# A two-layer streaming encoder step on one core: the gathered rows and the dense stage's middle rows get padded rows, so that each k starts at another distance from the weights

## The chip, the cores and the metric

The kernel runs on one core of one Trainium2 chip. The time is the device time of one execution in microseconds (us). TensorE is called PE in the rows, its weight loads PEld, VectorE DVE, ScalarE ACT, GpSimd POOL.

## The reference, cut to what matters

Two layers over 320 tokens (256 of a prompt, 64 of a running stream), model width 1024, everything in float32. Each layer mixes tokens (a short convolution beside a gated linear attention) between one input and one output projection, normalises, and then mixes channels: layer 0 with a dense SwiGLU of width 3584, layer 1 with 8 experts of the same width of which each token uses two.

```python
def _swiglu(x, w_gate, w_up, w_down):
    return (jax.nn.silu(x @ w_gate) * (x @ w_up)) @ w_down

def _moe(x, router, w_gate, w_up, w_down):
    ...
    logits = (xf @ router).astype(jnp.float32)
    top_v, top_i = lax.top_k(logits, TOP_K)
    gates = jax.nn.softmax(top_v, axis=-1)
    ...
    for e in range(N_EXPERTS):
        y = y + combine[:, e:e + 1] * _swiglu(xf, w_gate[e], w_up[e], w_down[e])
```

## The kernel before, in words

**Products in three parts.** A float32 product is made of three matmuls on rounded operands (type fp32r): high part by high part, and each high part by the other operand's rest. `raw` is a ring of 6 weight units of 2048 words per partition that SP loads; ScalarE rounds a unit into the ring `whi` (3 units), VectorE writes the rest into `wlo` (3 units), and TensorE reads both.

**Mixer and dense stage (16 + 42 + 16 units).** The weights are the stationary operand (128 x 128, loaded before each matmul), the tokens' transposed activations `xh`, `xl` (or `y_split`) the moving one with 320 columns. `split_product` (lines 619 to 625) issues the three matmuls of a pair: line 622 high by high, 623 high weights by low input, 624 low weights by high input. In the dense stage (`dense_mixer`) a chunk of 512 middle columns takes four gate and up units and two down units; the down units' moving operand is `hh[:, k, :]` and `hl[:, k, :]`, k from 0 to 3, which ScalarE (line 1258) and VectorE (line 1695) write.

**Expert stage.** Four passes of `pair` (experts two at a time, 128 gathered rows each, 14 chunks of 512 middle columns a pass). Here the gathered rows are the stationary operand and the weights the moving one, with 512 columns:

```python
for j in range(4):
    k = 4 * half + j
    ...
    wh, wl = slot(whi, n, SPLIT, 4)[:, j, :], slot(wlo, n, SPLIT, 4)[:, j, :]
    xh_k, xl_k = (xg[:, k, m, P * a:P * a + P] for m in range(2))
    pe.matmul(bank[:], xh_k, wh, start=k == 0, stop=False)                # line 959
    pe.matmul(bank[:], xh_k, wl, start=False, stop=False)                 # line 960
    mm = pe.matmul(bank[:], xl_k, wh, start=False, stop=k == KT - 1)      # line 961
```

A chunk is gate (24 matmuls), up (24), and the down product of the chunk before (24, line 984, stationary `hT_hi`/`hT_lo`, moving `whi`/`wlo`), with four transposes of 128 columns (line 997) between the two halves of the gate. At the end of a pass four gathers (line 934) make the next pass's `xg`: ScalarE evicts the high part (`hi_of_pair`, line 1297), VectorE the rest (`lo_of_pair`, line 1851). The order on each engine is written out by hand; semaphores tie the engines together.

**Where the operands lie.** Within a partition, `xg` has 2048 bytes a k (high part of 256 words, then the low part; expert `a` 512 bytes in). A unit of `whi` or `wlo` is 8192 bytes: in the expert gate and up units a k is 2048 bytes, in the dense down units too, in the mixer and the dense gate and up units 1024 bytes. `xh`, `xl`, `y_split`, `hh` and `hl` have 320 words, 1280 bytes, a k. Tiles start at multiples of 32 bytes. `raw`, `whi`, `wlo`, `xh`, `hh`, `hl`, `xg` and `hT_hi` all start 128 bytes past a multiple of 256. `w_split`, the stationary operand of the low-rank product (lines 800 and 801), has 128 bytes a k and starts behind `prm`, whose 110 words are rounded to 448 bytes, so it lies 32 bytes off the others' raster of 64.

Of the kernel before, what the change touches and what calls it, by code (L numbers as in the profile page):

```python
# [17 lines left out]
F32 = mybir.dt.float32  # L18
F32R = mybir.dt.float32r
I32 = mybir.dt.int32  # L20
ALU = mybir.AluOpType
ACT = mybir.ActivationFunctionType
AXX = mybir.AxisListType.X

P = 128
# [8 lines left out]
def hybrid_stream_step(nc, x_prompt, x_sample, cache_conv, state_gla, ln_mix_g, ln_mix_b, w_in, w_alpha2,  # L34
# [3 lines left out]
    DEPTH, D, IN_COLS = w_in.shape  # L38
    SEQ, DEC = x_prompt.shape[1], x_sample.shape[1]
    T = SEQ + DEC  # L40
# [4 lines left out]
    E = moe_router.shape[2]  # L45
# [3 lines left out]
    KT = D // P  # L49
    TT = -(-T // P)  # L50
# [70 lines left out]
    with ctx:  # L121
# [54 lines left out]
        def sbm(name, shape, dt=F32):  # L176
# [11 lines left out]
                                                                                        k=KT)  # L188
# [22 lines left out]
        def sbd(name, shape, dt=F32):  # L211
            return dense.enter_context(nc.sbuf_tensor(name, shape, dt))

        silu_g = sbd("silu_g", [P, 2, T])
        hid = sbd("hid", [P, 2, T])
        hh = sbd("hh", [P, 4, T], F32R)
        hl = sbd("hl", [P, 4, T], F32R)
        dense.close()
        early.close()
        late = ExitStack()  # L220
# [2 lines left out]
        def sbl(name, shape, dt=F32):  # L223
            return late.enter_context(nc.sbuf_tensor(name, shape, dt))

        def sbx(stack, name, shape, dt=F32):
            return stack.enter_context(nc.sbuf_tensor(name, shape, dt))
# [12 lines left out]
        acc_s.close()  # L240
        y_out = sbl("y_out", [P, TT, D])
        pair_s = ExitStack()
        xg = sbx(pair_s, "xg", [P, KT, 2, 2 * P], F32R)
        pair_s.close()
        ys_hi = sbl("ys_hi", [P, D], F32R)
        ys_lo = sbl("ys_lo", [P, D], F32R)
        sbl("xg_rest", [P, KT * 4 * P - 2 * D])
        sg = sbl("sg", [P, 2, 512])
        hm = sbl("hm", [P, 2, 512])
        hT_hi = sbl("hT_hi", [P, 2, 4, P], F32R)  # L250
# [2 lines left out]
        gT_hi = sbl("gT_hi", [P, TT * P], F32R)  # L253
# [13 lines left out]
        comb = sbl("comb", [P, TT, E])  # L267
        qpos = sbl("qpos", [P, TT, E])
        over_n = sbl("over_n", [P, 2 * E])
        over_k = sbl("over_k", [P, 3])  # L270
        src_at = sbl("src_at", [P, SRC])
        src_on = sbl("src_on", [P, SRC])
        slot_of = sbl("slot_of", [P, ROOM, SRC])
# [6 lines left out]
        row_in = sbl("row_in", [P, TT, SLOTS])  # L280
        row_at = sbl("row_at", [P, 3, TT])
        gate_at = sbl("gate_at", [P, 3, TT])
        in_6 = sbl("in_6", [P, TT])
        row_i = sbl("row_i", [P, 3, TT], I32)
        ctl_f = sbl("ctl_f", [P, 16])
        ctl = sbl("ctl", [1, 16], I32)
        rs_tok = sbl("rs_tok", [P, TT])
        acc_sum = sbl("acc_sum", [P, TT])
        ys_sums = sbl("ys_sums", [P, 4])
        ys_sum = sbl("ys_sum", [P, 1])  # L290
        sq_sums = sbl("sq_sums", [P, TT, 2])
        neg_mean = sbl("neg_mean", [P, TT])
        eps_1 = sbl("eps_1", [P, TT])
        pick_g = x[:, :, :].rearrange("p k t -> p (k t)")[:, 2 * D:2 * D + TT * P].rearrange("p (t s) -> p t s", t=TT)
        gb_rows = x[:, :, :].rearrange("p k t -> p (k t)")[:, 0:2 * D].rearrange("p (a d) -> p a d", a=2)
        lgT = hm[0:E, 0, 0:T]
# [321 lines left out]
        def _(pe):  # L618
# [320 lines left out]
            def pair(i, steps, first=False):  # L939
                unit, job = 0, GATHERS  # L940
                for part, c, half in steps:
# [3 lines left out]
                    if part in ("gate", "up"):  # L945
# [7 lines left out]
                        for j in range(4):  # L953
                            k = 4 * half + j
                            if j % 2 == 0:
                                pe.wait_ge(lo_ready, upto(2 * n + j // 2 + 1, i, 2 * PER_PAIR))
                            wh, wl = slot(whi, n, SPLIT, 4)[:, j, :], slot(wlo, n, SPLIT, 4)[:, j, :]
                            xh_k, xl_k = (xg[:, k, m, P * a:P * a + P] for m in range(2))
                            pe.matmul(bank[:], xh_k, wh, start=k == 0, stop=False)  # L959
                            pe.matmul(bank[:], xh_k, wl, start=False, stop=False)  # L960
                            mm = pe.matmul(bank[:], xl_k, wh, start=False, stop=k == KT - 1)  # L961
                            if j % 2:
                                mm.then_inc(unit_used, 1)
# [70 lines left out]
            def combine():  # L1034

                def newest(d, t):
                    out, tokens = ps[OUT_BANKS[t][d]][:], slice(P * t, P * t + P)
                    pe.matmul(out, gT_hi[:, tokens], ys_hi[:, HALVES[d]], start=False, stop=False)
                    pe.matmul(out, gT_lo[:, tokens], ys_hi[:, HALVES[d]], start=False, stop=False)
                    pe.matmul(out, gT_hi[:, tokens], ys_lo[:, HALVES[d]], start=False, stop=True).then_inc(r_tok, 1)  # L1040

                pe.wait_ge(ys_lo_ready, 1)
                for t in range(TT):
                    newest(0, t)

                pe.wait_ge(sum_ready, 1)
                for t in range(TT):
                    tokens = slice(P * t, P * t + P)
                    pe.matmul(ps[4][:, t:t + 1], gT_hi[:, tokens].bitcast(F32), ys_sum[:], start=True, stop=False)
                    mm = pe.matmul(ps[4][:, t:t + 1], gT_lo[:, tokens].bitcast(F32), ys_sum[:], start=False, stop=True)  # L1050
                mm.then_inc(mean_tok, 1)
                pe.wait_ge(ys_lo_ready, 2)
                for t in range(TT):
                    newest(1, t)
# [17 lines left out]
        def _(act):  # L1072
# [221 lines left out]
                act.activation(ident_r[:], ident[:], ACT.Copy).then_inc(ys_ready, 1)  # L1294

            def hi_of_pair(g, bank):
                act.activation(xg[:, 2 * g:2 * g + 2, 0, :], bank[:].rearrange("p (k s) -> p k s", k=2), ACT.Copy
                               ).then_inc(xg_hi_ready, 1)

            def pair(i, steps, first=False):  # L1300
# [77 lines left out]
        def _(dve):  # L1378
# [342 lines left out]
            def router():  # L1721
# [22 lines left out]
                    return n  # L1744

                dve.wait_ge(stored, 16 * LAYER_STORES * DEPTH)
                dve.memset(acc_sum[:], 0.0).then_inc(m_hid, 1)
                step(dve.memset(lg[:], 0.0))
                dve.wait_ge(lg_done, 1)
                step(dve.tensor_copy(lgT, ps[0][0:E, 0:T]))  # L1750
# [97 lines left out]
                    table(g_tab, csh)  # L1848

            def lo_of_pair(g, bank):  # L1850
                dve.tensor_tensor(xg[:, 2 * g:2 * g + 2, 1, :], bank[:].rearrange("p (k s) -> p k s", k=2),
                                  xg[:, 2 * g:2 * g + 2, 0, :].bitcast(F32), ALU.subtract).then_inc(job_read, 1)

            def make_pick(i, tab=q_tab):

# [5 lines left out]
            def rows_of_tokens(c, step):  # L1861
# [14 lines left out]
                elif c == 1:  # L1876
                    step(dve.scalar_tensor_tensor(out=g_tab[:], in0=row_of[:], scalar=0.0, in1=g_tab[:], op0=ALU.is_gt,
                                                  op1=ALU.mult))
                    step(dve.tensor_reduce(row_2, row_of[:], AXX, ALU.max))
                    step(dve.tensor_reduce(row_1, row_of[:], AXX, ALU.add))  # L1880
                    step(dve.tensor_tensor(row_1, row_1, row_2, ALU.subtract))
                    step(dve.tensor_tensor(row_in[:], row_of[:], row_2.unsqueeze(2).to_broadcast(full), ALU.is_equal))
                    step(dve.tensor_tensor(row_in[:], row_in[:], g_tab[:], ALU.mult))
                elif c == 2:
                    step(dve.tensor_reduce(gate_2, row_in[:], AXX, ALU.add))
                    step(dve.tensor_reduce(gate_1, g_tab[:], AXX, ALU.add))
                    step(dve.tensor_tensor(gate_1, gate_1, gate_2, ALU.subtract))
                    step(dve.tensor_scalar(in_6[:], qpos[:, :, E - 2], 1.0, None, ALU.is_ge))
                    step(dve.scalar_tensor_tensor(out=in_6[:], in0=qpos[:, :, E - 2], scalar=float(P), in1=in_6[:],
                                                  op0=ALU.is_le, op1=ALU.mult))  # L1890
                    step(dve.scalar_tensor_tensor(out=row_6, in0=qpos[:, :, E - 2], scalar=over_k[:, 1:2], in1=in_6[:],
                                                  op0=ALU.add, op1=ALU.mult))
                elif c == 3:
                    step(dve.tensor_tensor(gate_6, comb[:, :, E - 2], in_6[:], ALU.mult))
                    step(dve.tensor_tensor(gate_1, gate_1, gate_6, ALU.add))
                    step(dve.tensor_tensor(row_1, row_1, row_6, ALU.add))
                    step(dve.tensor_scalar(row_at[:], row_at[:], -1.0, 0.0, ALU.add, ALU.max))
                    dve.tensor_copy(row_i[:], row_at[:]).then_inc(rows_known, 1)
                elif c == 4:
                    for t in range(TT):  # L1900
                        ins = dve.tensor_scalar(pick_g[:, t, :], slot_no[:], qpos[:, t, E - 1:E], comb[:, t, E - 1:E],
                                                ALU.is_equal, ALU.mult)
                    ins.then_inc(rows_known, 1)
# [57 lines left out]
            def final_norm():  # L1961
                halves = [slice(512 * d, 512 * d + 512) for d in range(2)]
                for d, cols in enumerate(halves):
# [2 lines left out]
                                             in1=ys_hi[:, cols].bitcast(F32), op0=ALU.mult, op1=ALU.subtract,  # L1966
                                             accum_out=ys_sums[:, 2 + d:3 + d]).then_inc(ys_lo_ready, 1)
                dve.wait_ge(ys_lo_ready, 2)
                dve.tensor_reduce(ys_sum[:], ys_sums[:], AXX, ALU.add).then_inc(sum_ready, 1)
                dve.tensor_scalar(acc_sum[:], acc_sum[:], -1.0 / D, None, ALU.mult).then_inc(sum_ready, 1)  # L1970
                dve.wait_ge(sum_ready, 2)
                dve.wait_ge(mean_tok, 1)
                dve.scalar_tensor_tensor(out=neg_mean[:], in0=ps[4][:, 0:TT], scalar=-1.0 / D, in1=acc_sum[:],
                                         op0=ALU.mult, op1=ALU.add).then_inc(mean_ready, 1)
                dve.wait_ge(mean_ready, 1)
                dve.wait_ge(gb_landed, 32)
# [65 lines left out]
```

## Time and profile before

| | |
|---|---|
| median of 3 runs | 1600.7 us (1599.65 to 1600.92) |
| the profiled execution's own time | 1599.57 us |
| its span, first to last instruction | 1597.9 us |
| PE busy | 1575.9 us, 99% of the span, 8661 matmuls |
| PEld busy | 1395.9 us (87%) |
| DVE / ACT busy | 1244.9 us (78%) / 1022.2 us (64%) |
| granted clock of TensorE | 0.998 of the full 2.4 GHz |

A matmul's own duration (389 ns for 512 columns) is longer than the time from its start to the next one's start, because matmuls are pipelined; what a stage costs is read from the starts. Weight loads run beside the matmul before.

### The profile page before, as it was taken

Reading aid. Unit: us, or ns where it says so; the run is one execution under the profiler, and the core shown is the slowest. Engines: PE = TensorE matmul, PEld = TensorE weight load, DVE = VectorE, ACT = ScalarE, POOL = GpSimd, SP = SyncE. Lnnn points to the kernel's source line nnn. Section 1 sums busy time; section 2 is a strip of 40 time slices with the busy share of each in tenths; the row PEclk is TensorE's granted clock in tenths of the full one; section 3 lists DMA queues with packets and bytes.
Section 4 is the critical chain, followed back from the end, with each engine's and each line's share of the span. In section 5 each row is a group of like instructions: output and inputs, shape, how many; then the busy total and the mean of one; then the engine's idle time right before and its main releaser. Section 6 shows DMA issues by size and latency. Waiting matters only on the chain.

```text
span 1597.9 us, 23664 instructions
## 1 busy us (share of the span) xinstructions
PE 1575.9 (99%) x8661; PEld 1395.9 (87%) x8661; DVE 1244.9 (78%) x1416; ACT 1022.2 (64%) x1178; POOL 45.1 (3%) x72
## 2 busy tenths in 40 slices
PE   9999999999999999999999999999999999999997
PEld 8998999999989998888888888888888888888885
DVE  5577545444575678999998989988988988998996
ACT  4454333333354557788787778777778777877875
POOL 1002000000030010000000000000000001000100
PEclk9999999999999999999999999999999999999999
DMA  9524644444434344999998999998999999999992
GB/s 284 185 80 139 237 158 144 145 157 136 154 106 132 106 139 164 376 373 386 370 383 329 383 370 375 381 382 320 381 380 365 385 379 350 382 395 378 389 394 77
DMA packets 226576, 445.40 MB, mean 279 GB/s; under 512 B 10547, under 2 KB 72705, under 8 KB 226433
## 3 DMA queue, kind: packets, MB, share of 16 engines
q1 hardware_dynamic: 224288, 434.16, 75.4%
q0 software_dynamic: 2192, 9.98, 1.7%
q8 instruction: 58, 0.95, 0.2%
q14 instruction: 38, 0.30, 0.1%
HBM read 438.59 MB, written 8.67 MB: 280 GB/s over the span
## 4 chain that ended last, share of the span: by engine, by line
PE 95%; DVE 3%; ACT 1%; issue 1%; DVEq 0%; POOL 0%; ACTq 0%; POOLq 0%
PE ps L984 18%; PE ps L959 12%; PE ps L961 12%; PE ps L960 12%; PE ps L622 11%; PE ps L623 11%; PE ps L624 11%; PE ps L997 1%; PE ps L934 1%; PE ps L654 1%; DVE wlo L1388 1%; DVE x L1471 1%; DVE xl L1462 0%; DVE x L1453 0%; PE ps L1029 0%
## 5 line engine op out<-in xcount | busy, mean ns | idle before, releaser
L1388 DVE TENSOR_TENSOR wlo<-raw,whi 128x1024 fp32r<-128x1024 f32 x672 | 778.5, 1220 | 43.8 <-ACT whi L1083 42.6
L1083 ACT ACTIVATE whi<-raw 128x1024 fp32r<-128x1024 f32 x672 | 676.9, 1055 | 60.8 <-PE ps L984 51.9
L959 PE MATMUL ps<-whi,xg 128*128 128x512 f32 x896 | 354.2, 395 | 0.0
L961 PE MATMUL ps<-whi,xg 128*128 128x512 f32 x896 | 349.8, 390 | 0.0
L960 PE MATMUL ps<-wlo,xg 128*128 128x512 f32 x896 | 349.2, 390 | 0.0
L622 PE MATMUL ps<-xh,whi 128*128 128x320 f32 x832 | 260.2, 313 | 4.5 <-DVE xl L1462 3.8
L1383 DVE TENSOR_TENSOR wlo<-raw,whi 128x2048 fp32r<-128x2048 f32 x73 | 167.4, 2295 | 124.8 <-ACT whi L1079 124.8
L624 PE MATMUL ps<-xh,wlo 128*128 128x320 f32 x832 | 257.3, 309 | 0.0
L623 PE MATMUL ps<-xl,whi 128*128 128x320 f32 x832 | 257.3, 309 | 0.0
L961 PEld LDWEIGHTS ps<-whi,xg 128*128 128x128 f32 x896 | 168.3, 188 | 35.7
L960 PEld LDWEIGHTS ps<-wlo,xg 128*128 128x128 f32 x896 | 168.5, 188 | 33.6
L959 PEld LDWEIGHTS ps<-whi,xg 128*128 128x128 f32 x896 | 168.4, 188 | 33.3
L1079 ACT ACTIVATE whi<-raw 128x2048 fp32r<-128x2048 f32 x73 | 139.1, 1906 | 60.6 <-PE ps L624 56.1
L622 PEld LDWEIGHTS ps<-xh,whi 128*128 128x128 f32 x832 | 156.2, 188 | 9.4 <-issue 4.2
L623 PEld LDWEIGHTS ps<-xl,whi 128*128 128x128 f32 x832 | 156.3, 188 | 0.2
L624 PEld LDWEIGHTS ps<-xh,wlo 128*128 128x128 f32 x832 | 156.2, 188 | 0.0
L984 PE MATMUL ps<-whi,hT_hi 128*128 128x512 f32 x440 | 135.6, 390 | 0.0
L984 PE MATMUL ps<-wlo,hT_hi 128*128 128x512 f32 x440 | 135.6, 389 | 0.0
L984 PE MATMUL ps<-whi,hT_lo 128*128 128x512 f32 x440 | 135.5, 389 | 0.0
L984 PEld LDWEIGHTS ps<-whi,hT_lo 128*128 128x128 f32 x440 | 82.6, 188 | 17.2
L984 PEld LDWEIGHTS ps<-wlo,hT_hi 128*128 128x128 f32 x440 | 82.6, 188 | 17.2
L1337 ACT ACTIVATE hT_hi<-ps 128x512 fp32r<-128x512 f32 x56 | 33.5, 599 | 99.9 <-PE ps L997 99.5
(327 smaller groups left out, 1496.5 us busy)
## 6 DMA issues: line engine op xcount, KB each, us to landing
raw<-in_moe_w_gate SPq DMA_DIRECT2D x112, 1024.0 KB, 7.5
raw<-in_moe_w_up SPq DMA_DIRECT2D x112, 1024.0 KB, 7.8
raw<-in_moe_w_down SPq DMA_DIRECT2D x112, 1024.0 KB, 7.3
raw<-in_w_in SPq DMA_DIRECT2D x23, 1024.0 KB, 6.2
raw<-in_ffn_w_gate SPq DMA_DIRECT2D x14, 1024.0 KB, 5.0
raw<-in_ffn_w_up SPq DMA_DIRECT2D x14, 1024.0 KB, 5.1
raw<-in_ffn_w_down SPq DMA_DIRECT2D x14, 1024.0 KB, 5.0
raw<-in_w_out SPq DMA_DIRECT2D x8, 1024.0 KB, 5.1
```

The lines of the kernel that those rows point to most:

```text
L622: pe.matmul(out, wh, hi, start=start and j == 0, stop=False)
L623: pe.matmul(out, wh, lo, start=False, stop=False)
L624: mm = pe.matmul(out, wl, hi, start=False, stop=stop and j == len(pairs) - 1)
L959: pe.matmul(bank[:], xh_k, wh, start=k == 0, stop=False)
L960: pe.matmul(bank[:], xh_k, wl, start=False, stop=False)
L961: mm = pe.matmul(bank[:], xl_k, wh, start=False, stop=k == KT - 1)
L984: mm = pe.matmul(ps[4 + d][:], hT[:, c % 2, k, :], slot(w, n, SPLIT, 2)[:, j, 512 * d:512 * d + 512], start=fc == 0 and k == 0 and hT is h ...
L1079: act.activation(flat(whi, n, SPLIT), flat(raw, n, RAW), ACT.Copy).then_inc(hi_ready, 2)
L1083: act.activation(part(whi, n, SPLIT, h), part(raw, n, RAW, h), ACT.Copy).then_inc(hi_ready, 1)
L1337: act.activation(hT_hi[:, c % 2, :, :].rearrange("p f s -> p (f s)"), bank[:], ACT.Copy).then_inc(hT_hi_ready, 1)
L1383: dve.tensor_tensor(flat(wlo, n, SPLIT), flat(raw, n, RAW), flat(whi, n, SPLIT).bitcast(F32), ALU.subtract).then_inc(lo_ready, 2)
L1388: dve.tensor_tensor(part(wlo, n, SPLIT, h), part(raw, n, RAW, h), part(whi, n, SPLIT, h).bitcast(F32), ALU.subtract).then_inc(lo_ready, 1)
```

## The change: padded rows, and small tiles put together

`xg` gets 16 more words a k (2112 bytes instead of 2048), with high and low parts side by side in one row of 4 x 128 words; its readers and writers address the same words in the new form. `hh` and `hl` get 16 more words a k (1344 bytes instead of 1280). `xg_rest`, which keeps the room of `xg`, grows with it, so all tiles behind it lie 512 bytes further on. Some small tiles are put together (`over_k` with `in_6`; `rs_tok`, `eps_1`, `neg_mean`, `acc_sum` and `sq_sums`; `ys_sums` with `ys_sum`), which frees bytes that rounding to 32 took. No instruction, wait, count or shape of an operand changes; `xh`, `xl`, `y_split`, `hT_hi`, `hT_lo` and the weight rings keep their steps.

```diff
-        hh = sbd("hh", [P, 4, T], F32R)
-        hl = sbd("hl", [P, 4, T], F32R)
+        hh = sbd("hh", [P, 4, T + 16], F32R)[:, :, 0:T]
+        hl = sbd("hl", [P, 4, T + 16], F32R)[:, :, 0:T]
...
-        xg = sbx(pair_s, "xg", [P, KT, 2, 2 * P], F32R)
+        xg = sbx(pair_s, "xg", [P, KT, 4 * P + 16], F32R)
...
-        sbl("xg_rest", [P, KT * 4 * P - 2 * D])
+        sbl("xg_rest", [P, KT * (4 * P + 16) - 2 * D])
...
-        over_k = sbl("over_k", [P, 3])
+        over_in = sbl("over_in", [P, 3 + TT])
+        over_k, in_6 = over_in[:, 0:3], over_in[:, 3:3 + TT]
...
+        rs_parts = sbl("rs_parts", [P, 6, TT])
+        rs_tok, eps_1, neg_mean, acc_sum = (rs_parts[:, n, :] for n in range(4))
+        sq_sums = rs_parts[:, 4:6, :].rearrange("p a t -> p (a t)").rearrange("p (t a) -> p t a", a=2)
+        ys_parts = sbl("ys_parts", [P, 5])
+        ys_sums, ys_sum = ys_parts[:, 0:4], ys_parts[:, 4:5]
...
-                            xh_k, xl_k = (xg[:, k, m, P * a:P * a + P] for m in range(2))
+                            xh_k, xl_k = (xg[:, k, P * (2 * m + a):P * (2 * m + a) + P] for m in range(2))
...
-                act.activation(xg[:, 2 * g:2 * g + 2, 0, :], bank[:].rearrange("p (k s) -> p k s", k=2), ACT.Copy
+                act.activation(xg[:, 2 * g:2 * g + 2, 0:2 * P], bank[:].rearrange("p (k s) -> p k s", k=2), ACT.Copy
...
-                dve.tensor_tensor(xg[:, 2 * g:2 * g + 2, 1, :], bank[:].rearrange("p (k s) -> p k s", k=2),
-                                  xg[:, 2 * g:2 * g + 2, 0, :].bitcast(F32), ALU.subtract).then_inc(job_read, 1)
+                dve.tensor_tensor(xg[:, 2 * g:2 * g + 2, 2 * P:4 * P], bank[:].rearrange("p (k s) -> p k s", k=2),
+                                  xg[:, 2 * g:2 * g + 2, 0:2 * P].bitcast(F32), ALU.subtract).then_inc(job_read, 1)
```

## Rows read from the trace of the kernel before

**Rows 1.** The page's chain that ended last: shares by engine, then by line.
```profile
PE 95%; DVE 3%; ACT 1%; issue 1%; DVEq 0%; POOL 0%; ACTq 0%; POOLq 0%
PE ps L984 18%; PE ps L959 12%; PE ps L961 12%; PE ps L960 12%; PE ps L622 11%; PE ps L623 11%; PE ps L624 11%; PE ps L997 1%; PE ps L934 1%; PE ps L654 1%; DVE wlo L1388 1%; DVE x L1471 1%; DVE xl L1462 0%; DVE x L1453 0%; PE ps L1029 0%
```

**Rows 2.** Waits of PE: who waited for whom, us in total, times, longest.
```profile
PE ps L622 <- DVE xl L1462: 3.8, 8, 1.2
PE ps L934 <- DVE xg L1851: 2.3, 3, 0.8
```

**Rows 3.** Tile xg, every use: nanoseconds min/median/max, first and last start.
```profile
L959 PEld LDWEIGHTS ps<-whi,xg x896: 186/188/192, 614.1 to 1564.9; 128*128 128x128 f32 x180
L960 PE MATMUL ps<-wlo,xg x896: 387/389/398, 614.5 to 1565.4; 128*128 128x512 f32 x180
L961 PE MATMUL ps<-whi,xg x896: 388/389/398, 614.7 to 1565.6; 128*128 128x512 f32 x180
L1297 ACT ACTIVATE xg<-ps x16: 597/597/598, 609.8 to 1336.0; 128x512 fp32r<-128x512 f32 x16
L1851 DVE TENSOR_TENSOR xg<-ps,xg x16: 691/692/694, 610.5 to 1336.6; 128x512 fp32r<-128x512 f32 x16
```

**Rows 4.** Timeline of PE, one expert up product: start, duration; line 959, k 0 to 7.
```profile
1132.65 0.39 PE L959 MATMUL ps<-whi,xg 128*128 128x512 f32 x1
...
1133.33 0.39 PE L959 MATMUL ps<-whi,xg 128*128 128x512 f32 x1
...
1134.01 0.39 PE L959 MATMUL ps<-whi,xg 128*128 128x512 f32 x1
...
1134.69 0.39 PE L959 MATMUL ps<-whi,xg 128*128 128x512 f32 x1
...
1137.41 0.39 PE L959 MATMUL ps<-whi,xg 128*128 128x512 f32 x1
...
1138.09 0.61 PE L984 MATMUL ps<-whi,hT_hi 128*128 128x512 f32 x2
```

**Rows 5.** Timeline of PE, a dense down unit: first and sixteenth of its matmuls.
```profile
180.67 0.31 PE L622 MATMUL ps<-hh,whi 128*128 128x320 f32 x1
...
182.87 0.31 PE L622 MATMUL ps<-hh,whi 128*128 128x320 f32 x1
```

**Rows 6.** Timeline of PE, low-rank product of layer 1: 16 matmuls, then the next unit.
```profile
469.50 0.31 PE L800 MATMUL ps<-xh,w_split 128*128 128x320 f32 x1
469.64 0.31 PE L801 MATMUL ps<-xl,w_split 128*128 128x320 f32 x1
...
471.84 0.31 PE L622 MATMUL ps<-xh,whi 128*128 128x320 f32 x1
472.28 0.31 PE L622 MATMUL ps<-xh,whi 128*128 128x320 f32 x1
```

**Rows 7.** Tiles hh, then hT_hi: their uses, min/median/max ns.
```profile
L622 PEld LDWEIGHTS ps<-hh,whi x224: 187/188/188, 180.5 to 447.6; 128*128 128x128 f32 x112
L622 PE MATMUL ps<-hh,whi x224: 308/309/310, 180.7 to 447.8; 128*128 128x320 f32 x112
L1337 ACT ACTIVATE hT_hi<-ps x56: 597/599/601, 628.8 to 1569.6; 128x512 fp32r<-128x512 f32 x56
L1950 DVE TENSOR_TENSOR hT_lo<-ps,hT_hi x56: 672/692/694, 631.3 to 1572.2; 128x512 fp32r<-128x512 f32 x56
```

**Rows 8.** Timeline of PE around the four transposes between the halves of a gate.
```profile
1126.74 0.39 PE L959 MATMUL ps<-whi,xg 128*128 128x512 f32 x1
...
1129.46 0.60 PE L997 MATMUL ps<-ident,hm 128*128 128x128 f32 x4
1129.82 0.48 PE L959 MATMUL ps<-whi,xg 128*128 128x512 f32 x1
1130.13 0.39 PE L960 MATMUL ps<-wlo,xg 128*128 128x512 f32 x1
1130.37 0.40 PE L961 MATMUL ps<-whi,xg 128*128 128x512 f32 x1
```

**Rows 9.** Line 1354, the small sums of the last norm.
```profile
L1354 ACT ACTIVATE eps<-sq_sums,cst x3: 294/294/294, 1586.9 to 1591.4; 128x1 f32<-128x1 f32 x2, 64x1 f32<-64x1 f32 x1
```

More of the change, by code:

```diff
@@ L282, in hybrid_stream_step @@
         gate_at = sbl("gate_at", [P, 3, TT])
-        in_6 = sbl("in_6", [P, TT])
         row_i = sbl("row_i", [P, 3, TT], I32)
@@ L286, in hybrid_stream_step @@
         ctl = sbl("ctl", [1, 16], I32)
[L287 to L293, printed above, removed]
+        rs_parts = sbl("rs_parts", [P, 6, TT])
[3 more added lines that the diff above has]
+        ys_sums, ys_sum = ys_parts[:, 0:4], ys_parts[:, 4:5]
         pick_g = x[:, :, :].rearrange("p k t -> p (k t)")[:, 2 * D:2 * D + TT * P].rearrange("p (t s) -> p t s", t=TT)
@@ L1048, in combine @@
                     tokens = slice(P * t, P * t + P)
-                    pe.matmul(ps[4][:, t:t + 1], gT_hi[:, tokens].bitcast(F32), ys_sum[:], start=True, stop=False)
-                    mm = pe.matmul(ps[4][:, t:t + 1], gT_lo[:, tokens].bitcast(F32), ys_sum[:], start=False, stop=True)
+                    pe.matmul(ps[4][:, t:t + 1], gT_hi[:, tokens].bitcast(F32), ys_sum, start=True, stop=False)
+                    mm = pe.matmul(ps[4][:, t:t + 1], gT_lo[:, tokens].bitcast(F32), ys_sum, start=False, stop=True)
                 mm.then_inc(mean_tok, 1)
@@ L1746, in router @@
                 dve.wait_ge(stored, 16 * LAYER_STORES * DEPTH)
-                dve.memset(acc_sum[:], 0.0).then_inc(m_hid, 1)
+                dve.memset(acc_sum, 0.0).then_inc(m_hid, 1)
                 step(dve.memset(lg[:], 0.0))
@@ L1887, in rows_of_tokens @@
                     step(dve.tensor_tensor(gate_1, gate_1, gate_2, ALU.subtract))
-                    step(dve.tensor_scalar(in_6[:], qpos[:, :, E - 2], 1.0, None, ALU.is_ge))
-                    step(dve.scalar_tensor_tensor(out=in_6[:], in0=qpos[:, :, E - 2], scalar=float(P), in1=in_6[:],
+                    step(dve.tensor_scalar(in_6, qpos[:, :, E - 2], 1.0, None, ALU.is_ge))
+                    step(dve.scalar_tensor_tensor(out=in_6, in0=qpos[:, :, E - 2], scalar=float(P), in1=in_6,
                                                   op0=ALU.is_le, op1=ALU.mult))
-                    step(dve.scalar_tensor_tensor(out=row_6, in0=qpos[:, :, E - 2], scalar=over_k[:, 1:2], in1=in_6[:],
+                    step(dve.scalar_tensor_tensor(out=row_6, in0=qpos[:, :, E - 2], scalar=over_k[:, 1:2], in1=in_6,
                                                   op0=ALU.add, op1=ALU.mult))
                 elif c == 3:
-                    step(dve.tensor_tensor(gate_6, comb[:, :, E - 2], in_6[:], ALU.mult))
+                    step(dve.tensor_tensor(gate_6, comb[:, :, E - 2], in_6, ALU.mult))
                     step(dve.tensor_tensor(gate_1, gate_1, gate_6, ALU.add))
@@ L1968, in final_norm @@
                 dve.wait_ge(ys_lo_ready, 2)
-                dve.tensor_reduce(ys_sum[:], ys_sums[:], AXX, ALU.add).then_inc(sum_ready, 1)
-                dve.tensor_scalar(acc_sum[:], acc_sum[:], -1.0 / D, None, ALU.mult).then_inc(sum_ready, 1)
+                dve.tensor_reduce(ys_sum, ys_sums, AXX, ALU.add).then_inc(sum_ready, 1)
+                dve.tensor_scalar(acc_sum, acc_sum, -1.0 / D, None, ALU.mult).then_inc(sum_ready, 1)
                 dve.wait_ge(sum_ready, 2)
                 dve.wait_ge(mean_tok, 1)
-                dve.scalar_tensor_tensor(out=neg_mean[:], in0=ps[4][:, 0:TT], scalar=-1.0 / D, in1=acc_sum[:],
+                dve.scalar_tensor_tensor(out=neg_mean, in0=ps[4][:, 0:TT], scalar=-1.0 / D, in1=acc_sum,
                                          op0=ALU.mult, op1=ALU.add).then_inc(mean_ready, 1)
```

## The prediction, made before the changed kernel was run

> **What bounds the kernel now.** I read the page's busy shares and its chain first: PE is busy 99% of the span, and 95% of the chain that ended last is PE's, with the expert stage's lines 959 to 961 and 984 at 54% and the split products of lines 622 to 624 at 33% [rows 1]. Then PE's own waits: the two largest sums are 3.8 us on `xl` in the norms and 2.3 us on `xg` at the three pass boundaries [rows 2]. So up to the last norm only one thing moves the time by more than a few microseconds: the interval from one matmul's start to the next one's. DVE (78%) and ACT (64%) have slack.
>
> That interval I take from the timeline. In an expert up product the first of each k's three matmuls starts at 1132.65, 1133.33, 1134.01, 1134.69, and so on to 1137.41 for k = 7, and the next product at 1138.09: eight equal steps of 0.68 us, 24 matmuls in 5.44 us, 226.7 ns each [rows 4]. In a dense down unit 15 intervals take 2.20 us, 146.7 ns each [rows 5]. The difference, 80.0 ns for 192 columns, is 2.4 columns a ns (the full 2.4 GHz, one column a clock), which puts 213.3 ns of the 226.7 and 133.3 of the 146.7 on the columns and leaves **13.3 ns a matmul** in both. If where the operands lie costs anything throughout, it must be in these 13.3 ns.
>
> **Does the distance enter there?** The change turns on one claim, that what a matmul costs depends on how far its stationary operand lies from its moving one. The kernel before already tries many distances:
> - Expert gate and up: `xg` and the weights both step by 2048 bytes a k, so the distance within a multiple of 2048 is one and the same for every k, half, slot and expert up to 512 (expert) and 1024 (low part). If that were a bad distance, all 24 matmuls would pay; they pay 13.3 ns [rows 4].
> - Dense down: `hh` steps by 1280, the weights by 2048; each k already lies 768 bytes from where the k before did. They pay 13.3 ns too [rows 5]; over all 224 of line 622, the load is 187 to 188 ns and the matmul 308 to 310 [rows 7].
> - Layer gates, ups and projections: `xh` steps by 1280, the weights by 1024, so the distance moves 256 bytes a k. Three matmuls from 471.84 to 472.28 make 0.44 us, 146.7 ns each [rows 6].
> - Low-rank product: `w_split` steps by 128 bytes and lies 32 bytes off the raster of 64. Each k's distance moves by 1280 - 128 = 1152 bytes, and no distance of this product is a multiple of 64. Its 16 matmuls take 469.50 to 471.84, 2.34 us, 146.3 ns each [rows 6], the same within the 0.01 us to which starts are printed.
>
> Four kinds of distance, one that is constant, one in steps of 768, one in steps of 256 and one off the raster, all give the same remainder within 0.6 ns. So the 13.3 ns goes with each matmul that follows a weight load and not with the distance. The load of `xg` is 186 to 192 ns over 896 uses of line 959 [rows 3], against 187 to 188 in the dense unit [rows 7], and both lie under the 226.7 ns interval.
>
> The Trainium skill bears on this at two places, which point in opposite ways. Its page "SBUF — State Buffer", section "Who interferes with whom", gives PE two read ports of its own, independent of each other, one for the moving operand and one for weight loads; by that rule the distance cannot matter and the sum is zero, as the rows have it. Its page "TensorE: Matmul & The Clock Gate", section "Wait — 56ns, not 53.3ns?", gives back-to-back matmuls N / 2.4 GHz plus about 2.5 ns, 215.7 ns at 512 columns; the trace disagrees with 226.7. By that figure some 10.8 ns a matmul would be open, an estimate of 3360 x 10.8 ns = 36 us for the matmuls whose distances this change moves.
>
> **The change part by part.**
> 1. *`xg` at 2112 bytes a k, for the 2688 matmuls of lines 959 to 961.* Value 0. Lower bound: all 13.3 ns go, 2688 x 13.3 = 35.8 us less. Upper bound: new distances bring a conflict, at the largest slowdown a matmul of these lines shows in sequence without transposes directly before it: 1130.13 to 1130.37, 0.24 us against 0.227, some 9 to 13 ns, say 10 [rows 8]; 26.9 us more if all had it. I take 0 because rows 4 to 6 are the nearest, and no two of them differ.
> 2. *`hh` and `hl` at 1344 bytes, for 672 matmuls (224 of each of lines 622 to 624).* Value 0, by the same argument; bounds -9.0 us (672 x 13.3 ns) and +6.7 us (672 x 10 ns).
> 3. *Writers of `xg`.* The four eviction pairs of a pass's end put a break of 1088 bytes instead of 1024 between two runs of 256 words. Whether there is a break at all costs nothing now: ACT takes 597 ns into `xg` in two runs [rows 3] and 599 ns into `hT_hi` in one; DVE 692 ns for both [rows 3, 7]. Value 0. PE does wait here, 2.3 us over three boundaries [rows 2]. Were both evictions twice as long, what PE waits for at a boundary would rise by at most the last pair's 0.60 + 0.69 = 1.3 us, four times 5.2 us with the router's; the other end is zero, as a shorter break saves no element.
> 4. *Writers of `hh`, `hl`.* Each writes 320 adjacent words of one k, as before; the instruction and its length stay. PE waits for neither in any row of note, so even some 50 ns more each would be hidden by the up and down units between.
> 5. *Tiles moved by 512 bytes, small tiles put together.* `sg`, `hm`, `hT_hi`, `hT_lo` and the rest keep their place in any raster up to 512. The small sums on the path lie in the last norm only, where the three of line 1354 take 294 ns each whatever the token tile and address [rows 9]. Value 0, bounds under 0.5 us on either side: the neighbours in the norm are a dozen instructions of this size, and 294 ns without a spread over three addresses leaves room for a few per cent of 12 x 0.29 = 3.5 us.
> 6. *Added or moved instructions, DMAs, waits:* none; no queue is reordered.
>
> The sum is 0. The profiled execution took 1599.57 us (span 1597.9 and 1.7 around it), 1.1 us under the median of the runs shown, 1600.7; the changed kernel should have its median where this one has it: **1600.5 us**. What a measurement of this kernel can tell from no change is about 0.2%, 3.2 us.
>
> **The rivals.**
> - *The remainder is a matter of place after all and goes (faster).* Then parts 1 and 2 give -35.8 - 9.0 = -44.8 us, 1555.9 us; half of it 1578. For: `xg` and the weights do move in step, and 13.3 ns is 32 clocks at 2.4 GHz, which is much for a change of weights. Against: the three other kinds of distance pay the same to the nanosecond. 4%.
> - *The slow stretch behind the transposes is a matter of place (faster).* A chunk's gate takes 1126.74 to 1132.65 = 5.91 us [rows 4, 8], against 5.44 for the up product; 0.36 of this are the four transposes, which leaves 0.11 us, mostly the matmul of 0.31 us at 1129.82 [rows 8]. Over 56 chunks that is 6.2 us; if the new distances of k = 4 to 7 cleared it, 1594.5 us. For: it does hit only these k. Against: the same k in the up product 5 us later show nothing [rows 4]; it follows the transposes. 3%.
> - *The change does not do what it says,* because padding leaves the distances equal where it counts: within a slot k moves by 64 bytes, so they do differ; but if the chip looks only at coarser rasters than 448 bytes (7 x 64), nothing moves. That time is the forecast's, and I keep it in it.
> - *New distances collide (slower).* Before, in the expert and dense stages every distance is a multiple of 256 (the one product off the raster is 32 aside, not 64). With 64 bytes a k, the odd k come to lie 64 bytes past a multiple of 128, which no row has tried. If the loads of these k met the moving reads and cost the 10 ns above, it would be 4 of 8 k in `xg`, 1344 x 10 ns = 13.4 us, and 2 of 4 in `hh`, 336 x 10 = 3.4 us: 1617.5 us. It decides from one k of eight on (336 matmuls, 3.4 us, 1604.1), since less is within 0.2%. For: nothing but that it is untried. Against: an operand 32 bytes off the raster in steps of 1152 shows no such cost in 16 matmuls [rows 6]. 5%.
>
> **How the numbers follow.** Forecast 88%, rivals 4, 3 and 5%. The forecast's own range is 1597.5 to 1603.5 (the shown runs spread 1.3 us; the rest is another chip, and part 5's and a little of part 3's bounds). The cases outside hold 12% together, so the range need not reach to them; I stretch it by half a microsecond below and above: 1597 to 1604. Faster by over 0.2% is the two fast rivals, and 1% that the median falls there by chance, 0.08; slower 0.06; the same 0.86.
>
> **What would show it.** In the trace after, the starts of line 959 should still lie 0.68 us apart for every k, 5.44 us for an up product; the dense down unit's 15 intervals still 2.20 us; loads 188 ns, matmuls 389 and 309; line 1297 at 597 ns and line 1851 at 692; the wait of line 934 on `xg` still 2.3 us. Gaps of less than 0.226 in lines 959 to 961 alone, with line 984 unchanged, would prove the first rival, since `hT` and its weights keep their places. Steps that alternate with k, longer for odd k, would prove the last. The forecast fails if any of the four kinds of distance was only by chance free of the effect, that is if the cost depends on steps of 64 bytes in a way that 32 plus multiples of 128 hides.

## The result: slower by 0.7%, and the profile after

The changed kernel takes 1612.3 us (median of 3 runs, 1611.46 to 1612.47) against 1600.7: ratio 1.0073, 95% interval 1.005 to 1.0096, a small loss but clear of the noise. It is outside the range that was given. The profiled execution took 1612.47 us, its span is 1610.8 us, 12.9 more than before.

Nothing in the page's first parts names a cause: PE is still busy 99% of the span with the same 8661 matmuls, and DVE and ACT do what they did. The chain is PE's as in [rows 1], by 96% now:

```profile
PE 96%; DVE 3%; issue 1%; ACT 0%; DMA 0%; SPq 0%; DVEq 0%; ACTq 0%
PE ps L982 18%; PE ps L958 13%; PE ps L957 13%; PE ps L959 13%; PE ps L620 11%; PE ps L621 11%; PE ps L622 11%; PE ps L932 2%; PE ps L995 1%; DVE x L1469 1%; DVE xl L1460 0%; PE ps L652 0%; DVE x L1451 0%; DMA proj<-in_x_prompt 0%; PE ps L1027 0%
```

PE's two largest waits are those of [rows 2], 3.8 and 2.3 us, to the tenth:

```profile
PE ps L620 <- DVE xl L1460: 3.8, 8, 1.2
PE ps L932 <- DVE xg L1849: 2.3, 3, 0.8
```

So no wait took the 12.9 us; the matmuls themselves must start further apart. The view that shows it quickest is PE by windows: the columns are the window, its length, PE's busy time with the number of matmuls in brackets, the granted clock, DMA share and GB/s. Before, then after:

```profile
100.00:600.00 500.00, 495.53 (x3410) 1.00 0.44 144
605.00:612.00 7.00, 6.52 (x52) 1.00 0.00 1
700.00:1500.00 800.00, 797.68 (x3669) 1.00 1.00 373
```

```profile
100.00:600.00 500.00, 495.52 (x3410) 1.00 0.44 144
605.00:612.00 7.00, 6.68 (x44) 0.76 0.01 2
700.00:1500.00 800.00, 797.69 (x3622) 1.00 1.00 368
```

From 100 to 600 us, mixers and dense stage with their padded `hh` and `hl`, the number is the same, 3410. In 800 us of the expert stage PE starts 47 matmuls fewer with the same busy time: 800 x (3669 / 3622 - 1) = 10.4 us. From its first to its last load of `xg` the stage takes 962.9 us (615.0 to 1577.9, in the tile view below) instead of 950.8 (614.1 to 1564.9 [rows 3]), 12.1 us more. It also starts 0.9 us later: a lower clock during the first gathers (0.76 in the window at 605) costs some 1.4 us there, of which the earlier stages, some 0.5 us ahead, give back a part. The clock is no part of the change, as the same window shows 0.76 in a kernel below that is as fast as before.

The timeline, as in [rows 4], now of the changed kernel: one chunk from its down product (two starts a row) over the gate to the up product and the next down product.

```profile
1128.56 0.63 PE L982 MATMUL ps<-whi,hT_hi 128*128 128x512 f32 x2
1129.03 0.62 PE L982 MATMUL ps<-wlo,hT_hi 128*128 128x512 f32 x2
1129.49 0.62 PE L982 MATMUL ps<-whi,hT_lo 128*128 128x512 f32 x2
...
1132.23 0.62 PE L982 MATMUL ps<-whi,hT_lo 128*128 128x512 f32 x2
1132.68 0.62 PE L982 MATMUL ps<-whi,hT_hi 128*128 128x512 f32 x2
...
1134.04 0.39 PE L957 MATMUL ps<-whi,xg 128*128 128x512 f32 x1
...
1134.72 0.40 PE L957 MATMUL ps<-whi,xg 128*128 128x512 f32 x1
...
1135.42 0.39 PE L957 MATMUL ps<-whi,xg 128*128 128x512 f32 x1
...
1140.03 0.40 PE L957 MATMUL ps<-whi,xg 128*128 128x512 f32 x1
...
1140.73 0.39 PE L957 MATMUL ps<-whi,xg 128*128 128x512 f32 x1
...
1145.59 0.40 PE L982 MATMUL ps<-whi,hT_hi 128*128 128x512 f32 x1
```

The up product takes 1140.03 to 1145.59, 5.56 us instead of 5.44, 231.7 ns a matmul instead of 226.7. The gate takes 5.99 instead of 5.91 to 5.93. The down product, whose operands the change doesn't touch, takes 5.48 instead of 5.44, and all of it at its beginning: its first pairs of starts are 0.47 and 0.46 us apart, its later ones 0.45. A disturbance that the up product leaves dies out in it within about 8 matmuls. The three together are some 0.22 us a chunk, 56 times 12 us.

The gate also shows where the slowing begins. Its first k, whose rows lie as before against the weights, takes 0.68 us (1134.04 to 1134.72), as in [rows 4]; its second, the first whose rows lie 64 bytes aside, takes 0.70 (to 1135.42).

The tile view, as in [rows 3]: the load of line 957 is still 186 to 193 ns, but the median matmul of line 958 went from 389 ns to 396, and the evictions kept their 598 and 692 ns.

```profile
L957 PEld LDWEIGHTS ps<-whi,xg x896: 186/188/193, 615.0 to 1577.9; 128*128 128x128 f32 x180
L958 PE MATMUL ps<-wlo,xg x896: 387/396/402, 615.4 to 1578.4; 128*128 128x512 f32 x180
L1295 ACT ACTIVATE xg<-ps x16: 597/598/601, 610.5 to 1346.0; 128x512 fp32r<-128x512 f32 x16
L1849 DVE TENSOR_TENSOR xg<-ps,xg x16: 691/692/695, 611.2 to 1346.6; 128x512 fp32r<-128x512 f32 x16
```

The dense down unit is as in [rows 5], 15 intervals in 2.20 us; the third line is the tile view of `hh`, as in [rows 7]:

```profile
180.27 0.31 PE L620 MATMUL ps<-hh,whi 128*128 128x320 f32 x1
...
182.47 0.31 PE L620 MATMUL ps<-hh,whi 128*128 128x320 f32 x1
L620 PE MATMUL ps<-hh,whi x224: 304/309/317, 180.3 to 447.2; 128*128 128x320 f32 x112
```

So these matmuls cost nothing more in sum, but the pad does reach them: their durations spread from 304 to 317 ns, where they were 308 to 310 before.

### The profile page after: what moved, and what is told of

Same layout as the page of the kernel before. It is cut to its first block, busy times and chain, and to the rows that moved or that the text cites. A ratio compares the mean times of both kernels' runs of the same rounds, so it can differ in the third digit from the quotient of the medians.

```text
span 1610.8 us, 23664 instructions
## 1 busy us (share of the span) xinstructions
PE 1589.1 (99%) x8661; PEld 1397.7 (87%) x8661; DVE 1245.7 (77%) x1416; ACT 1022.9 (64%) x1178; POOL 45.6 (3%) x72
## 4 chain that ended last, share of the span: by engine, by line
PE 96%; DVE 3%; issue 1%; ACT 0%; DMA 0%; SPq 0%; DVEq 0%; ACTq 0%
PE ps L982 18%; PE ps L958 13%; PE ps L957 13%; PE ps L959 13%; PE ps L620 11%; PE ps L621 11%; PE ps L622 11%; PE ps L932 2%; PE ps L995 1%; DVE x L1469 1%; DVE xl L1460 0%; PE ps L652 0%; DVE x L1451 0%; DMA proj<-in_x_prompt 0%; PE ps L1027 0%
## 5 line engine op out<-in xcount | busy, mean ns | idle before, releaser
L958 PE MATMUL ps<-wlo,xg 128*128 128x512 f32 x896 | 354.3, 395 | 0.0
L982 PEld LDWEIGHTS ps<-whi,hT_hi 128*128 128x128 f32 x440 | 82.3, 188 | 18.1
```

The source lines that it names most:

```text
L982: mm = pe.matmul(ps[4 + d][:], hT[:, c % 2, k, :], slot(w, n, SPLIT, 2)[:, j, 512 * d:512 * d + 512], start=fc == 0 and k == 0 and hT is h ...
```

## The experiments

All are forms of the changed kernel. A ratio is to the kernel before, run on the same chip, with its 95% interval.

### Which part: `hh_only` and `xg_only`

```diff
-        xg = sbx(pair_s, "xg", [P, KT, 4 * P + 16], F32R)     # hh_only
+        xg = sbx(pair_s, "xg", [P, KT, 4 * P + 0], F32R)
-        hh = sbd("hh", [P, 4, T + 16], F32R)[:, :, 0:T]       # xg_only, hl alike
+        hh = sbd("hh", [P, 4, T + 0], F32R)[:, :, 0:T]
```

> Only hh and hl at 1344 bytes a k, xg back at 2048; the small tiles stay joined. Theory A (the cost comes with xg's distance to the weights moving by 64 bytes from k to k) and theory B (it comes with rows of xg lying off the raster of 256 bytes) both expect the time of the kernel before, 1600.7 us within 2 us, since the dense stage of the changed kernel took as long as before. Theory C (joined small tiles) expects 1612 us; so would a cost of hh and hl that the trace hides.

> Only xg at 2112 bytes a k, hh and hl back at 1280. A and B expect the whole loss, 1612 us, an expert up product of 24 matmuls at 5.60 us instead of 5.44. If hh has a share, less than 1612.

Measured: `hh_only` 1600.26 us, ratio 1.0001 (0.9991 to 1.001); `xg_only` 1612.86 us, 1.0077 (1.0061 to 1.0094). The loss is `xg`'s alone. The small tiles, joined in both, cost nothing.

### Stepped distance or any odd distance: `xg_base64` and `xg_pad256`

```diff
+        xg_m = sbx(pair_s, "xg", [P, 4224], F32R)             # xg_base64: 2048 bytes a k, 64 bytes later
+        xg = xg_m[:, 16:16 + KT * 4 * P].rearrange("p (k c) -> p k c", k=KT)
+        xg = sbx(pair_s, "xg", [P, KT, 4 * P + 64], F32R)     # xg_pad256: 2304 bytes a k
```

> xg at 2048 bytes a k but started 64 bytes later; its tile keeps the larger room, so all tiles behind lie 512 bytes further on as in the changed kernel. Theory A expects 1600.7 us within 2 and 5.44 us an up product, since every k again has the same distance. Theory B expects at least the loss of the changed kernel, 1612 us or more, since now every k and not three of four lies off the raster. Theory C' (the tiles moved by 512 bytes) expects 1612.

> xg at 2304 bytes a k, so each k lies 256 bytes further from the weights than the one before; two small tiles of the router lie over ys to make room. Theory A in its plain form (any change of distance from k to k costs) expects 1612 us. Theory A with a raster of 256 bytes (only the distance modulo 256 counts) and theory B expect 1600.7 within 2. The pattern of gaps in the changed kernel repeats every 4 k, which speaks for the raster of 256.

Measured: `xg_base64` 1616.05 us, ratio 1.0099 (1.0082 to 1.0116); `xg_pad256` 1599.89 us, 0.9999 (0.999 to 1.0009). My theory A, that the distance must change from k to k to cost, fell: a constant distance that is 64 bytes off costs more. (Theory C', the tiles moved by 512 bytes, isn't told apart by `xg_base64`, which moves them too. `xg_pad256` moves them by 2048 bytes for nothing, and `w_pad` below, which leaves them where they were against `xg`, is slow.) An up product of `xg_base64`, first start to the next product's:

```profile
1142.33 0.39 PE L958 MATMUL ps<-whi,xg 128*128 128x512 f32 x1
...
1147.92 0.62 PE L983 MATMUL ps<-whi,hT_hi 128*128 128x512 f32 x2
```

5.59 us, 233 ns a matmul: 6 ns more in every one. And a step of 256 bytes a k, a changing distance, costs nothing, so only the remainder modulo 256 counts. What was left: the distance (modulo 256), or the place of one of the two operands by itself.

### The distance or an operand's own place: `both_pad`, `w_pad`, `all_by64`

```diff
+        whi = sb("whi", [P, SPLIT * 4 * (512 + 16)], F32R)    # both_pad and w_pad; wlo alike,
+                            wh, wl = wcut(whi, n, 4, j, slice(0, 512)), wcut(wlo, n, 4, j, slice(0, 512))
...
-        raw = sb("raw", [P, RAW * UNIT])                      # all_by64
+        raw = sb("raw", [P, RAW * UNIT + 16])
```

To make room, `lrT` and `rowsT` lie over `state` and `given` in these three, and in the first two the router's comparison tables over `ys`.

> xg at 2112 bytes a k as in the changed kernel, and whi and wlo padded too: 2112 bytes for each 512 words. In gate and up, xg and weights now move together, so the distance modulo 256 is 0 for every k as in the kernel before, while both operands lie off the raster. In the expert down product the weights' rows move by 64 bytes and hT_hi, hT_lo don't. Theory D (the distance modulo 256 decides) expects an up product at 5.44 us and a down product at about 5.56, 56 times 0.12 more, 1607 us. Theory E (the stationary rows' own place decides) expects up 5.56, down 5.44, 1612 us. Theory F (the moving rows' own place) expects both slow, 1618 us.

> Only whi and wlo padded to 2112 bytes for each 512 words, xg at 2048 bytes a k as before. Theory D expects gate, up and down all slow, up and down at about 5.56 us, 1618 us. Theory E expects the time of before, 1600 us, since the stationary rows lie as before. Theory F expects 1618. With both_pad: D is the only one that has gate and up fast there and slow here.

> Every tile behind raw starts 64 bytes later (whi, wlo, xh, hh, xg, hT_hi all now 192 bytes past a multiple of 256), with xg at 2048 bytes a k; all distances between tiles are those of the kernel before. If it is the place of each operand on the raster that decides (all of them at 128 past a multiple of 256 in the kernel before), 1615 us as with xg_base64. If it is how load and stream lie to each other, in the sense that the load of the next matmul runs beside the stream of this one, 1600 us.

Measured: `both_pad` 1616.36 us, ratio 1.01 (1.0084 to 1.0117); `w_pad` 1616.87 us, 1.0104 (1.0087 to 1.0121); `all_by64` 1600.36 us, 1.0002 (0.9992 to 1.0011). Up product, down product and the gate's start of `both_pad`:

```profile
1124.73 0.40 PE L970 MATMUL ps<-whi,xg 128*128 128x512 f32 x1
...
1126.12 0.40 PE L970 MATMUL ps<-whi,xg 128*128 128x512 f32 x1
...
1127.51 0.40 PE L970 MATMUL ps<-whi,xg 128*128 128x512 f32 x1
...
1128.90 0.40 PE L970 MATMUL ps<-whi,xg 128*128 128x512 f32 x1
...
1130.29 0.63 PE L995 MATMUL ps<-whi,hT_hi 128*128 128x512 f32 x2
...
1135.87 0.39 PE L970 MATMUL ps<-whi,xg 128*128 128x512 f32 x1
```

and an up product of `all_by64`, then its windows at the first gathers and in the expert stage:

```profile
1117.09 0.39 PE L957 MATMUL ps<-whi,xg 128*128 128x512 f32 x1
...
1122.53 0.62 PE L982 MATMUL ps<-whi,hT_hi 128*128 128x512 f32 x2
```

```profile
605.00:612.00 7.00, 6.82 (x45) 0.76 0.01 2
700.00:1500.00 800.00, 797.68 (x3669) 1.00 1.01 373
```

`all_by64` moves every operand of PE off its old place and keeps every distance between them (only `raw`, which PE doesn't read, stays): 5.44 us an up product, 3669 matmuls in the window, the same as before. So E and F, the own place of an operand, are out; what counts is relative. (`w_pad` alone speaks against E, with `xg` where it was and slow, and `xg_base64` against F, with the weights where they were.) (Its lower clock at 605 us is the one seen after the change, in a span of 1599.2 against the 1597.7 of `xg_pad256`, which has 1.00 there: 1.5 us that belong to neither layout.) But D in its simple form missed too: `both_pad` keeps each matmul's own two operands at 0 modulo 256 in gate and up, and its up product is slow all the same, 5.56 us. Nor is that handed on from the slow down product before: it goes on in four equal steps of 1.39 us for six matmuls each (1124.73, 1126.12, 1127.51, 1128.90, 1130.29), and doesn't die out. What does differ there is the pair that runs together. The timeline of the kernel before shows that each load starts with the matmul ahead of it, at 1129.01 both:

```profile
1129.01 0.39 PE L960 MATMUL ps<-wlo,xg 128*128 128x512 f32 x1
1129.01 0.19 PEld L961 LDWEIGHTS ps<-whi,xg 128*128 128x128 f32 x1
```

The load for k + 1 runs beside the stream of k, and in `both_pad` these two lie 64 bytes off, once in three matmuls; with a disturbance that lasts some 8 matmuls, as in the down product above, once in three is enough to never be rid of it. That explains `both_pad`, and fits all the others; no kernel here tested it by itself, so it stays the reading that is left, not one shown.

### How far off, and how finely: `xg_base32`, `xg_base128`, `xg_pad128`

```diff
+        xg = xg_m[:, 8:8 + KT * 4 * P].rearrange("p (k c) -> p k c", k=KT)    # xg_base32; xg_base128: 32
+        xg = sbx(pair_s, "xg", [P, KT, 4 * P + 32], F32R)                     # xg_pad128
```

> xg at 2048 bytes a k, started 32 bytes later: the distance of the low-rank product's w_split, which cost nothing with 320 columns. If 32 bytes aside costs nothing with 512 columns either, 1600 us, and only multiples of 64 that aren't multiples of 256 are bad. If it costs, 1607 to 1616 us, and what the prediction read from products of 320 columns did not hold for 512.

> xg at 2048 bytes a k, started 128 bytes later. If the raster is 128 bytes, 1600 us; if it is 256 bytes, as the period of 4 k in the changed kernel says, slower, between 1607 and 1620 us.

> xg at 2176 bytes a k, 128 bytes more than the weights. Since a constant 128 bytes (xg_base128) cost 5.59 us an up product, this should be slow too, 1608 to 1614 us, with a pattern that repeats every 2 k instead of every 4. If the pattern is not of 2 k, the raster of 256 bytes that the changed kernel's period of 4 k suggests is wrong.

Measured: 1615.14 us, ratio 1.0094 (1.0077 to 1.0111); 1613.35 us, 1.0083 (1.0066 to 1.0099); 1611.3 us, 1.0074 (1.0057 to 1.0091). The same window of the expert stage, in this order:

```profile
700.00:1500.00 800.00, 797.68 (x3609) 1.00 0.99 367
```

```profile
700.00:1500.00 800.00, 797.69 (x3616) 1.00 1.00 367
```

```profile
700.00:1500.00 800.00, 797.68 (x3625) 1.00 1.00 369
```

A constant 32, 64 or 128 bytes off all cost, 60, 61 and 53 matmuls of 3669 (the 61 from the same window of `xg_base64`); being nearer buys little. `xg_base32` lies 32 bytes off the raster of 64, as `w_split` does, on which I had relied: with 512 columns it does cost. (The two distances aren't the same modulo 256: 32 for `xg_base32`, 224 and 96 in turn for `w_split`.) For `xg_pad128`, which has 44 matmuls fewer, the slowing came as expected, but the starts of line 956 within an up product don't repeat every 2 k. Such a period isn't set by the layout alone: in an up product of `xg_base128`, whose distance is constant, the interval after the 1st, 8th, 15th and 22nd matmul is 241 ns and the others 228 to 233 (means over 46 chunks of its trace, the last one left out). So the period of 4 k in the changed kernel proves little by itself, and the raster of 256 bytes rests on `xg_pad256` and the three bases.

### Why the dense stage is spared: `down512`, `down512_pad` and shorter ones

The dense down product reads 512 columns instead of 320; what the further columns give is used nowhere.

```diff
-                        mm = split_product(ps[4 + m][:, 0:T], [(wh, wl, hh[:, k, :], hl[:, k, :])], k == 0, k == 3)
+                        mm = split_product(ps[4 + m][:], [(wh, wl, hh_m[:, 336 * k:336 * k + 512], hl_m[:, 336 * k:336 * k + 512])], k == 0, k == 3)
```

(320 for 336 in `down512`; the second unit alike; 352, 384 and 448 for 512 in the last three.)

> Control for the next: the 672 matmuls of the dense down product read 512 columns instead of 320 (the 192 beyond a k's row are of no use and go to columns of the bank that nobody reads), hh and hl at 1280 bytes a k. Both theories expect 226.7 ns from start to start there, 672 x 80 ns more than before, 1654 us.

> The same with hh and hl at 1344 bytes a k. If products of 320 columns were spared because of their length, these 672 matmuls of 512 columns now take some 231 to 233 ns, 3 to 5 us more than down512. If they were spared because the weights are the stationary operand there, 226.7 ns as in down512.

> down512_pad with 352 columns a matmul in the dense down product, hh and hl at 1344 bytes a k. Without a cost 352 / 2.4 + 13.3 = 160.0 ns from start to start. If the cost grows with the columns from 320 on, 161; if it sets in whole above some length, either 160 or 165.

> The same with 384 columns. Without a cost 173.3 ns; growing with the columns between 320 and 512, 175; whole, 173.3 or 178.

> The same with 448 columns. Without a cost 200.0 ns; growing with the columns, 204; whole, 200 or 205.5.

Measured: `down512` 1666.98 us, 13 more than expected, of which 11.8 are a wait for `hl` that I made stricter for the wider reads; `down512_pad` 1670.43 us, 3.4 more. The second down unit of a chunk, 48 matmuls, first start and the start behind, in `down512` and then in `down512_pad`:

```profile
193.25 0.39 PE L622 MATMUL ps<-hh,whi 128*128 128x512 f32 x1
...
204.12 0.30 PE L622 MATMUL ps<-xh,whi 128*128 128x320 f32 x1
```

```profile
193.45 0.39 PE L622 MATMUL ps<-hh,whi 128*128 128x512 f32 x1
...
204.57 0.30 PE L622 MATMUL ps<-xh,whi 128*128 128x320 f32 x1
```

10.87 us against 11.12: 226.5 ns and 231.7. With the weights stationary the product pays as `xg` does once it is long enough; which operand is which doesn't matter, the number of columns does. With 352 columns the unit takes 7.78 us, 162.1 ns where 160.0 would be free of cost:

```profile
190.09 0.33 PE L622 MATMUL ps<-hh,whi 128*128 128x352 f32 x1
...
197.87 0.32 PE L622 MATMUL ps<-xh,whi 128*128 128x320 f32 x1
```

With 448 columns:

```profile
192.00 0.37 PE L622 MATMUL ps<-hh,whi 128*128 128x448 f32 x1
...
201.71 0.31 PE L622 MATMUL ps<-xh,whi 128*128 128x320 f32 x1
```

9.71 us, 202.3 ns against 200.0. With 384:

```profile
190.49 0.33 PE L622 MATMUL ps<-hh,whi 128*128 128x384 f32 x1
...
198.95 0.30 PE L622 MATMUL ps<-xh,whi 128*128 128x320 f32 x1
```

8.46 us, 176.2 ns against 173.3. So the cost is there from 352 columns on, 2 to 3 ns up to 448 and 5 at 512: neither expectation (growing from 320 in proportion, or whole) is right. These three lengths have one execution each and no control at 1280 bytes a k; what they are held against is worked out from the 13.3 ns that 320 and 512 columns share.

## Why the prediction was wrong, point by point

- **What bounds the kernel** held: PE's interval from start to start is what moved, and nothing else.
- **The step that failed** is the one headed "Does the distance enter there?". It read from four kinds of distance that the interval doesn't depend on it. Three of them (the expert product's constant distance, the gates' steps of 256 and `hh` with its 768) are the same case modulo 256, and it is the good one; the remainder of 13.3 ns says nothing of the others. The fourth, `w_split`, was truly off the raster, but with 320 columns, and `hh_only` and `down512_pad` show that this length is spared what 512 pays; `xg_base32`, also 32 bytes off the raster of 64, loses 0.94%. I carried a reading from 320 columns over to 512 without a row for it. Nor was the length a small matter in the rows themselves: I wrote that the loads' 188 ns lie under the interval of 226.7 ns, which is so, but at 320 columns they are longer than the interval of 146.7 ns, so a load there outlasts the time that one matmul takes. Whether this is why 320 columns are spared was not tested.
- **Part 1** (`xg`, value 0, upper bound +26.9 us) measured 0.12 us an up product and 0.06 to 0.08 a gate, some 10 to 11 us in 56 chunks; the price I named for a conflict, 10 ns a matmul, was above the 5 ns that it is here, and above the 6 to 7 of the constant distances. **Part 5** had the down product untouched; it pays 0.04 us a chunk, 2 us in all, for what the up product hands on.
- **Part 2** (`hh`, value 0) came out at 0, but not because the distance does nothing: the durations spread more widely, and at 320 columns their sum stays. **Parts 3, 4 and 6** held: 598 and 692 ns, and 2.3 us of waiting as before.
- **The slow rival** named the right kind of cause, loads that meet the moving reads, and gave it 5%. It put the cost on the odd k alone and on `hh` too, 1617.5 us; in truth all k pay, less each, and `hh` nothing. "For: nothing but that it is untried" should have weighed more: every row of the expert stage was at one distance modulo 256. The slow stretch behind the transposes [rows 8], which I held to be theirs alone, looks like the same kind of disturbance: gaps of 0.23 to 0.24 us that die out where the distance is good, as in the down product after the change. No run here tested that it is the same.
- The **fast rivals** are out: at 512 columns no product in any kernel here got below some 226.5 ns a matmul.
- The Trainium skill's page "SBUF — State Buffer", section "Who interferes with whom", has PE's two read ports independent, with nothing said of where the operands lie. Measured, the relative place of the two operands costs 5 to 7 ns of 227 at 512 columns, so that sentence isn't the whole story, and I was wrong to let it stand beside the rows as agreement. The other page that I drew on, the Trainium skill's "TensorE: Matmul & The Clock Gate", section "Wait — 56ns, not 53.3ns?", has some 2.5 ns over the columns' own time; here it is 13.3 in every good layout with a weight load before each matmul.

No experiment points to a version faster than the kernel before: `hh_only`, `xg_pad256` and `all_by64` equal it. Left open: what in the chip the raster of 256 bytes is, why the cost depends on the number of columns as it does, and whether it is the load beside the stream, as `both_pad` suggests.

## What to carry to other kernels

Where fp32r matmuls of more than 320 columns run back to back with a weight load each, give the rows of both operands steps that are multiples of 256 bytes, and start both at the same remainder modulo 256. That each matmul's own two rows have the same remainder is not enough: `both_pad` has it in gate and up, and its up product is as slow as the changed kernel's. A pad of 64 bytes cost 0.7% on `xg` and nothing on rows read with 320 columns, and one of 256 cost nothing. An interval that is the same in many places of a profile proves only that these places share a condition: before calling a cost absent, name what they have in common (here modulo 256, or the length) and look for a row that differs in just that. When busy time and waits stand still and the time moves, count instructions in a window of fixed length.

## What the runs showed of the hardware that was not expected

- The start-to-start time of a 128x512 fp32r matmul with its own weight load is 226.7 ns with all rows of both operands at 0 modulo 256 bytes of each other, and about 233 ns at a constant 32, 64 or 128 bytes; moving all tiles together by 64 bytes changes nothing.
- A disturbance outlives its cause: the down product, whose distances are good, starts at some 231 ns a matmul behind the changed kernel's up product and is back at 227 after 8 matmuls; behind the up product of `xg_base64` it is back after 3 (means over 47 chunks).
- 320 columns are spared: 3410 matmuls in 500 us with and without the pad of `hh` and `hl`, though single durations spread from 304 to 317 ns instead of 308 to 310; with the weights' rows padded instead (`w_pad`) 3414.
- The granted clock drops in the first gathers (0.76 from 605 to 612 us) in some executions and not in others, whatever the layout: `xg_base128`, slow, keeps 1.00 there, and `all_by64`, fast, doesn't. It is worth some 1.1 to 1.4 us, about the spread of the runs.
